# The last down-projection block of a decoder step: tokens stationary, the closing layer norm inside it

## The reference

```
x = layer_norm(ALPHA * x + h @ w_out, ln1_g, ln1_b)
u = relu(x @ w_up)
y = layer_norm(ALPHA * x + (u * u) @ w_down, ln2_g, ln2_b)

def layer_norm(x, g, b):
    mu = mean(x);  var = mean(square(x - mu))
    return (x - mu) * rsqrt(var + 1e-5) * g + b
```

## Time and profile before

| | |
|---|---|
| median of 3 runs | 2955.85 us |
| span of the profiled execution | 2953.3 us |
| PE busy | 2803.1 us (95%) |
| DVE busy | 1887.3 us (64%) |
| ACT busy | 842.9 us (29%) |
| POOL busy | 207.3 us (7%) |
| last sum of block 31 starts | 2906.40 us |
| last store issued | 2950.38 us |

### The profile page before, as it was taken

How to read it: one execution, slowest core, us unless ns; L and a number is a source line. 1 busy time by engine, 2 the same in 40 slices (tenths; PEclk the granted TensorE clock), 3 DMA queues, 4 the chain that set the end, 5 groups by cost and what they waited for, 6 DMA issues and landing times. The chain is left out here.

```text
span 2953.3 us, 58897 instructions
## 1 busy us (share of the span) xinstructions
PE 2803.1 (95%) x25775; PEld 2658.4 (90%) x25775; DVE 1887.3 (64%) x2204; ACT 842.9 (29%) x1226; POOL 207.3 (7%) x226
## 2 busy tenths in 40 slices
PE   7999999999999887899899999999999999999995
PEld 7998889888887665899789999999999999999994
DVE  3264555455553685536877777777777777777775
ACT  2221222122212355213533233232232322322321
POOL 2011101110110321001000000000000000000003
PEclk9999999999999899999999999999999999999997
DMA  9489999999999722445122232332323323323222
GB/s 343 154 314 402 410 374 412 411 400 394 413 396 340 246 79 82 104 132 138 51 79 86 86 114 71 103 106 67 115 84 88 109 72 107 101 71 115 79 94 89
DMA packets 340851, 548.62 MB, mean 186 GB/s; under 512 B 20940, under 2 KB 244781, under 8 KB 330019
## 3 DMA queue, kind: packets, MB, share of 16 engines
q1 hardware_dynamic: 263682, 334.37, 34.0%
q0 software_dynamic: 13872, 141.28, 11.8%
q10 hardware_dynamic: 63040, 69.21, 6.9%
HBM read 508.96 MB, written 35.84 MB: 184 GB/s over the span
## 5 line engine op out<-in xcount | busy, mean ns | idle before, releaser
L2129 DVE SCALAR_TENSOR_TENSOR base<-big_G,base 128x544 f32<-128x544 f32 x512 | 369.6, 722 | 244.3 <-PE big_G L1964 244.3
L449 PE MATMUL prj_G<-prj_xh,prj_wh 128*128 128x280 f32 x1696 | 504.0, 297 | 20.8 <-DVE prj_wl L692 13.9
L451 PE MATMUL prj_G<-prj_xh,prj_wl 128*128 128x280 f32 x1696 | 498.5, 294 | 0.0
L450 PE MATMUL prj_G<-prj_xl,prj_wh 128*128 128x280 f32 x1696 | 497.8, 294 | 0.0
L699 DVE STREAM_TRANSPOSE prj_kT<-base 128x4096 f32<-128x4096 f32 x64 | 284.5, 4445 | 258.3 <-PE prj_S L482 258.3
L2041 ACT ACTIVATE wh<-raw 128x1024 fp32r<-128x1024 f32 x227 | 239.4, 1059 | 652.8 <-PE big_G L1964 542.8
L1962 PE MATMUL big_G<-ff_uh,wh 128*128 128x272 f32 x1360 | 392.3, 288 | 3.6 <-DVE base L2129 3.5
L1963 PE MATMUL big_G<-ff_ul,wh 128*128 128x272 f32 x1360 | 393.5, 289 | 0.0
L1964 PE MATMUL big_G<-ff_uh,wl 128*128 128x272 f32 x1360 | 393.4, 289 | 0.0
L449 PEld LDWEIGHTS prj_G<-prj_xh,prj_wh 128*128 128x128 f32 x1696 | 322.9, 190 | 46.3 <-issue 34.5
L2116 DVE TENSOR_TENSOR wl<-raw,wh 128x1024 fp32r<-128x1024 f32 x227 | 277.0, 1220 | 86.3 <-ACT wh L2041 86.3
(11 more groups left out here) (418 smaller groups left out, 6097.2 us busy)
## 6 DMA issues: line engine op xcount, KB each, us to landing
prj_v_nat<-in_cache_v SPq DMA_DIRECT2D x242, 512.0 KB, 7.6
raw<-in_w_down SPq DMA_DIRECT2D x128, 512.0 KB, 4.4
raw<-in_w_up SPq DMA_DIRECT2D x120, 512.0 KB, 4.4
prj_raw<-in_w_in ACTq DMA_DIRECT2D x103, 512.0 KB, 17.6
raw<-in_w_out SPq DMA_DIRECT2D x16, 1024.0 KB, 7.1
prj_scratch<-prj_stage ACTq DMA_DIRECT2D x53, 280.0 KB, 9.3
out_xr<-x_scratch SPq DMA_DIRECT2D x16, 544.0 KB, 4.0
base<-in_cache_v SPq DMA_DIRECT2D x14, 512.0 KB, 7.2
```

Of the source, the lines that this page charges most:

```text
L449: mm(out, w_hi[:, k, m], xh[:, k0 + k, cols], start=(first and k == 0), stop=False)
L450: mm(out, w_hi[:, k, m], xl[:, k0 + k, cols], start=False, stop=False)
L451: last = mm(out, w_lo[:, k, m], xh[:, k0 + k, cols], start=False, stop=(end and k == nk - 1))
L2129: V.scalar_tensor_tensor(out, G[2 + t % 2][:, :, 0:HALF_M], 1.0 / ALPHA, out, ALU.mult, ALU.add).then_inc(y_done, 1)
```

## The change

The first 31 blocks stay as they are. The last block's down product is done by `down_last`, with the tokens stationary: for each of the four prompt token tiles t and each quarter d of the features (512 columns, one PSUM bank), six float32r matmuls with 512 moving columns of w_down, and behind them four float32 matmuls that turn the four pieces of `y` into the same bank, against `ident_a`, the identity times ALPHA. The bank thus holds the whole ALPHA * x + u2 @ w_down, with tokens on partitions, and no add on VectorE is needed. The fourth weight piece has buffers of its own (`fourth_h`, `fourth_l`).

The 32 samples are done ahead of it by `samples` in plain float32, with the four feature quarters on four groups of 32 partitions of one bank (8 matmuls of 512 columns, 16 turns); their mean and variance over the four quarters are made by two one-column matmuls against `select` (`over_quarters`).

`phase_end` is gone. Its work is done tile by tile behind `down_last`, with four output tiles in place of two. Gain and offset, and their quarters for the samples (ten loads), are issued on SP right after the last weight load, and land in the space of `xh`. The banks of tiles 0 and 2 are one set, of 1 and 3 the other; tile t (from 2) waits for the norm of tile t - 2. VectorE's order per tile is: last two banks' statistics, moments, scale, first two banks' statistics of the next tile, gain. GpSimd adds the offset for tiles 0 to 2. For tile 3, ScalarE normalises four quarters, VectorE does gain and offset of each, and SP stores each.

```diff
+            def samples():
+                pe.wait_ge(relu_done, NBLK)
...
+                pe.wait_ge(y_done, KT * LAST_BLK)
+                for k in range(FB):
+                    for d in range(DOWN):
+                        mm(SAMPLE[NS * d:NS * (d + 1), :], u2[:, k, NT * P:TM], down_raw(d)[:, k, :], start=(k == 0), stop=False)
+                pe.wait_ge(end_act, ACT_AT["ident_a"])
+                for j in range(4):
+                    for d in range(DOWN):
+                        last = mm(SAMPLE[NS * d:NS * (d + 1), j * P:(j + 1) * P], y[:, 4 * d + j, NT * P:TM], ident_a, start=False, stop=(j == 3))
+            def down_last(base):
+                samples()
+                pe.wait_ge(low_done, NLOW + LAST_BLK)
...
+                for t in range(NT):
+                    if t >= 2:
+                        pe.wait_ge(end_act, ACT_AT[f"norm {t - 2}"])
+                    for d in range(DOWN):
+                        if t == 0:
+                            pe.wait_ge(lo_done, base + d + 1)
+                        if t == 1 and d == 3:
+                            pe.wait_ge(end_dve, DVE_AT["scale s"])
...
+                        for k in range(FB):
+                            mm(bank, uh[:, k, tokens(t)], w_hi[:, k, :], start=(k == 0), stop=False)
+                            mm(bank, ul[:, k, tokens(t)], w_hi[:, k, :], start=False, stop=False)
+                            mm(bank, uh[:, k, tokens(t)], w_lo[:, k, :], start=False, stop=False)
+                        for j in range(4):
+                            last = mm(bank[:, j * P:(j + 1) * P], y[:, 4 * d + j, tokens(t)], ident_a, start=False, stop=(j == 3))
+                        last.then_inc(down_ps, 1)
+                        if t == 0 and d == 2:
+                            pe.wait_ge(end_act, ACT_AT["rows"])
+                            pe.wait_ge(end_dve, DVE_AT["moments s"])
+                            over_quarters(0, mv_s[:, 0:1])
+                        if t == 1 and d == 0:
+                            pe.wait_ge(end_dve, DVE_AT["square s"])
+                            over_quarters(1, mv_s[:, 3:4])
-            down(NBLK - 1, base, base)
+            down_last(FIRST + NCH * (NBLK - 2))
```

On ScalarE:

```diff
-            high(base + 3, BY_FREE[3], 2 * NBLK - 2, downs=downs + 20)
+            ac.wait_ge(raw_full[BY_FREE[3]], 16 * (2 * NBLK - 2))
+            ac.wait_ge(up_done, DOWN + UP * (NBLK - 2))
+            A(fourth_h, Q[BY_FREE[3]], ACT.Copy).then_inc(hi_done, 1)
+            A(ident_a, ident[:, :], ACT.Copy, scale=ALPHA).then_inc(end_act, 1)
...
+            ac.wait_ge(sample_ps, PE_AT["rows"])
+            A(rows, SAMPLE, ACT.Copy).then_inc(end_act, 1)
+            ac.wait_ge(sample_ps, PE_AT["var"])
+            A(mv_s[:, 4:5], MEAN[:, 1:2], ACT.Sqrt, bias=eps).then_inc(end_act, 1)
+            deviation(0)
+            ac.wait_ge(end_dve, DVE_AT["scale s"])
+            A(out_s, rows, ACT.Identity, scale=mv_s[:, 4:5], bias=mv_s[:, 5:6]).then_inc(end_act, 1)
+            normalise(0)
+            for t in (1, 2):
+                deviation(t)
+                normalise(t)
+            deviation(3)
+            ac.wait_ge(end_dve, DVE_AT["scale 3"])
+            for d, cols in enumerate(QUARTERS):
+                A(out[3][:, cols], X[1][d], ACT.Identity, scale=mv[:, 6:7], bias=mv[:, 7:8]).then_inc(end_act, 1)
```

On VectorE and GpSimd:

```diff
+            def scale(t):
+                s = 4 * (t % 2)
+                dv.wait_ge(end_act, ACT_AT[f"sd {t}"])
+                step(V.reciprocal(mv[:, s + 2:s + 3], mv[:, s + 2:s + 3]))
+                V.scalar_tensor_tensor(mv[:, s + 3:s + 4], mv[:, s:s + 1], -1.0, mv[:, s + 2:s + 3], ALU.mult, ALU.mult).then_inc(end_dve, 1)
...
+            scale(0)
+            statistics(1, (0, 1))
+            dv.wait_ge(end_act, ACT_AT["norm s"])
+            V.tensor_tensor(out_s, out_s, gain_s, ALU.mult).then_inc(end_dve, 1)
+            dv.wait_ge(end_dve, DVE_AT["gain s"])
+            V.tensor_tensor(out_s, out_s, offset_s, ALU.add).then_inc(end_dve, 1)
+            times_gain(0)
+            for t in (1, 2):
+                step(statistics(t, (2, 3)))
+                moments(t)
+                scale(t)
+                statistics(t + 1, (0, 1))
+                times_gain(t)
+            step(statistics(3, (2, 3)))
+            moments(3)
+            scale(3)
+            for d, cols in enumerate(QUARTERS):
+                dv.wait_ge(end_act, ACT_AT[f"norm 3.{d}"])
+                V.tensor_tensor(out[3][:, cols], out[3][:, cols], gain[:, cols], ALU.mult).then_inc(end_dve, 1)
+                dv.wait_ge(end_dve, DVE_AT[f"gain 3.{d}"])
+                V.tensor_tensor(out[3][:, cols], out[3][:, cols], offset[:, cols], ALU.add).then_inc(end_dve, 1)
...
+            po.wait_ge(up_done, DOWN + UP * (NBLK - 2))
+            G_.memset(eps, LN_EPS).then_inc(end_pool, 1)
+            for i in range(2):
+                G_.tensor_tensor(part_sum[:, NS * i:NS * (i + 1)], ident[:, 2 * NS * i:2 * NS * i + NS], ident[:, 2 * NS * i + NS:2 * NS * (i + 1)],
+                                 ALU.add).then_inc(end_pool, 1)
...
+            for t in range(NT - 1):
+                po.wait_ge(end_dve, DVE_AT[f"gain {t}"])
+                G_.tensor_tensor(out[t], out[t], offset, ALU.add).then_inc(end_pool, 1)
```

More of the change, by code:

```diff
@@ L1900, in phase_ff, with over @@
         PRODUCTS = ((0, B11), (1, B21), (3, T4), (3, T2), (0, T1), (2, T3), (1, B22))
+        NT, WIDE = 4, 512
+        def over(name, shape, at, dt=F32):
+            return nc.alloc_sbuf_tensor_at("ff_" + name, shape, dt, offset=at)
+        gain, offset = (over(f"vec{i}", [P, D], big["xh_at"] + 4 * i * D)[:, :] for i in range(2))
+        gain_s, offset_s, rows, out_s = (over(f"sample{i}", [P, WIDE], big["xh_at"] + 8 * D + 4 * i * WIDE)[:, :] for i in range(4))
+        ident_a, select, part_sum, mv, mv_s, eps = (
+            over(x, [P, n], big["xh_at"] + 8 * D + 16 * WIDE + 4 * at)[:, :]
+            for x, n, at in (("ident_a", P, 0), ("select", P, P), ("part_sum", 96, 2 * P), ("mv", 8, 3 * P), ("mv_s", 8, 3 * P + 8), ("eps", 1, 3 * P + 16)))
@@ L1920, in tile, with down_raw, tokens @@
             return (t + KH) % KT if b == 0 else t
+        def down_raw(d):
+            return flat(Q[BY_FREE[d]]).rearrange("p (k n) -> p k n", k=FB)
+        def tokens(t):
+            return slice(P * t, P * (t + 1))
         @block.sync
@@ new lines, in _, with statistics, moments @@
+            dv.wait_ge(hi_done, base + 4)
+            V.tensor_tensor(fourth_l, Q[BY_FREE[3]], fourth_h.bitcast(F32), ALU.subtract).then_inc(lo_done, 1)
+            step = Chain(dv, dve)
+            def statistics(t, banks):
+                for d in banks:
+                    dv.wait_ge(down_ps, KT * LAST_BLK + DOWN * t + d + 1)
+                    ins = V.bn_stats(stats[:, d, :], X[t % 2][d])
+                return ins
+            def moments(t):
+                s = 4 * (t % 2)
+                V.bn_aggr(mv[:, s:s + 2], flat(stats[:, :, :])).then_inc(end_dve, 1)
@@ new lines, in _ @@
+            dv.wait_ge(small_in, 16 * 2 * (1 + DOWN))
+            dv.wait_ge(end_act, ACT_AT["rows"])
+            step(V.bn_stats(stats_s[:, 0, :], rows))
+            V.bn_aggr(mv_s[:, 0:2], stats_s[:, 0, :]).then_inc(end_dve, 1)
+            statistics(0, (0, 1))
+            dv.wait_ge(sample_ps, PE_AT["mean"])
+            dv.wait_ge(end_dve, DVE_AT["moments s"])
+            step(V.tensor_tensor(mv_s[:, 2:3], mv_s[:, 0:1], MEAN[:, 0:1], ALU.subtract))
+            V.scalar_tensor_tensor(mv_s[:, 3:4], mv_s[:, 2:3], mv_s[:, 2:3], mv_s[:, 1:2], ALU.mult, ALU.add).then_inc(end_dve, 1)
@@ new lines, in _ @@
+            step(statistics(0, (2, 3)))
+            moments(0)
+            dv.wait_ge(end_act, ACT_AT["sd s"])
+            step(V.reciprocal(mv_s[:, 4:5], mv_s[:, 4:5]))
+            V.scalar_tensor_tensor(mv_s[:, 5:6], MEAN[:, 0:1], -1.0, mv_s[:, 4:5], ALU.mult, ALU.mult).then_inc(end_dve, 1)
+            scale(0)
[3 more added lines that the diff above has]
+            dv.wait_ge(end_dve, DVE_AT["gain s"])
```

165 lines of the change are left out of this document (72 added, 93 removed), and 3 rows, old and new, of the table DVE_AT.

## The result

The changed kernel takes 2938.81 us (median of 4 runs, 2929.57 to 2944.21), the one before 2958.26 (4 runs, 2951.85 to 2960.85; the three given above and one more). The ratio is 0.9928, with a 95% interval of 0.9901 to 0.9956: by it about 21 us less, by the two medians 19.5. Forecast were 23.9 less, a ratio of 0.9919.

A forecast was written before the change was run, and what follows sets the result against it. TensorE bounds the feed-forward phase; behind it VectorE and GpSimd take turns for 46.2 us. Handover, block, a 9.05 us norm loop and last tile end at 2929.45 instead of 2953.3, 23.9 less: 2932.0 on the median, range 2924 to 2938.

The forecast's parts named there:

- Handover: Before the last block's down product: the samples' matmuls run in TensorE's gap; block starts at 2880.45, 0.35 us later than before.
- The hidden loads: Ten gain and offset loads, issued on SP behind the last weight load, 15 us ahead of the closing norm: costed at nothing.
- The block: Last block's down product: 24 matmuls at 0.226 and 16 turns at 0.12, 7.35 us a tile, 29.4 for four.
- rival 2: Turns in the last block and samples: each costs 0.107 us more, everything 3.0 later, time 2935.0; chance 0.07.
- The clock: Start of the last block: the dip to the 1.2 GHz level after TensorE's gap stays, costing 1.6 us.
- The hold: Closing norm: the next tile's two-SBUF-operand scale on VectorE waits until GpSimd's offset ends, making a loop of 9.05 us a tile.
- Last tile: Tile 3 after its scale: first quarter's norm 0.6, eight VectorE pieces 5.5, last store 2.9 us, ending at 2929.45.
- rival 1: Closing norm: scale and offset run side by side without a hold, TensorE is the bound, time 2925.1; chance 0.11.
- 3: Last block: the clock stays at 1.2 GHz throughout, the block takes 54.8 us, time 2949.4; chance 0.05.
- 4: Last block: stationary loads no longer overlap the matmuls, 86 us in place of 29.4, time 2982, slower; chance 0.02.
- What was said to prove me wrong: Scales taking 0.16 beside a running offset, TensorE waiting microseconds for norm 1 or samples' moments, or block clock 0.5 over 4 us.
- What was said to prove me right: Block start near 2880.5, matmuls every 0.226, turns 0.11 to 0.12, scales ending with offsets, offsets 9.05 apart, about 6 us last.

The follow-up runs named there:

- e6: Changed kernel with a one-operand scale and three of four turns per quarter left out in tiles 1 to 3: tail 47.39 us, against 54.55 for the changed kernel.
- e9: Changed kernel with the prompt tiles' turns in TensorE's transpose mode, ahead of the float32r matmuls, two-operand scale kept: tail 51.74 us against 54.55.
- e2: Changed kernel with the samples' matmuls waiting for the low half of u, so TensorE idles as before the change: tail 58.05 us against 54.55.
- e4: Changed kernel with the last tile normalised, multiplied, added by GpSimd and stored whole instead of in pieces: tail 59.30 us against 54.55.
- e1: Changed kernel with each tile's scale using one SBUF tensor operand, the other a per-partition scalar: tail 51.75 us against 54.55.
- e7: Changed kernel with the prompt tiles' turns in transpose mode and the one-operand scale: tail 45.82 us against 54.55.
- e3: Changed kernel with three of four turns per quarter left out in tiles 1 to 3, 36 of 64: tail 53.30 us against 54.55.
- e10: As e8, but in the last tile all four centring pieces come before the four finishing ones: tail 45.22 us, ratio 0.9892 to the kernel before.
- e8: As e7, with the last tile's norm on VectorE alone, centring and finishing pieces interleaved: tail 45.24 us, ratio 0.9896 to the kernel before.
- e5: Changed kernel with VectorE alone doing the prompt tiles' norm, without ScalarE's norm and GpSimd's additions: tail 50.56 us, ratio 0.9932 to the kernel before.

## Why the prediction was right, and where it was 2.4 us off

By its own steps, all from the anchor:

- *Handover.* Block start 3.2, measured 3.6: right. The samples' eight matmuls took 1.92 us and not 1.0 to 1.3, for the reason below, but most of that lay under the wait for `ident_a`; their turns took 1.0 instead of 0.5, and that, with `ident_a` 0.1 early, is the 0.4. TensorE's gap was filled.
- *The hidden loads.* Costed at nothing, and nothing shows: no wait for them stands ahead of any instruction. No run moves them back.
- *The block.* The step that failed: "20 fp32 matmuls of 129 columns took 2.47 us, so 0.12 each at most". The x20 counts ten matmuls. A plain fp32 matmul leaves two rows in the trace, as the x8 for four turns shows, and costs about twice what I read: 0.23 for 128 columns. So a tile takes 9.15 us instead of 7.35. It is rival 2 (chance 0.07), whose size, 0.107 more a turn, was right; e6 (0.225 a turn) and e9 (0.11 once the turn is one row) show it. The Trainium skill (FP8 and Floating Point Precision, "TensorE Precision Notes") gives true fp32 four passes, by which, as an estimate, 128 columns at 2.4 GHz would be 0.21 us; the trace agrees (0.225), and my reading of the earlier trace rows against it was wrong. The same miscount gave the samples' matmuls, priced from the x8 row, which is four matmuls. In the pace the miscount cost nothing, as rival 2 had worked out, but only by a narrow margin: a tile of 9.15 is 0.2 shorter than the loop of the hold.
- *The clock.* I kept a dip of 1.6 us, and there was none; e2 shows why. It hid most of the dearer first tile: gain 0 started at 20.0, predicted 18.2. From the block's start to gain 0 it was 16.4 where I had 15.0 with the dip and 13.4 without: 3.0 more, 24 x 0.107 = 2.6 of it for turns and the rest for matmuls every 0.232 instead of 0.226 (36 of them) and the two small products of the samples. So the dip that did not come offset the step that failed: without this luck the miss would have been 4.0 and not 2.4 us. With 0.4 from the handover and less 1.6 of dip that is the 1.8. (e9, with cheap turns, starts gain 0 2.9 earlier.)
- *The hold.* Right in mechanism and nearly in size: all three scales end within 0.02 of an addition's end; the loop is 9.34 instead of 9.05. The differences are the norm, which is two instructions of 1024 columns here, 2.30 instead of 2.06, and the addition (4.59, 4.58 and 4.50 instead of 4.50). Over two rounds that is the other 0.6. Scale 3 ended at 45.6, predicted 43.2: 1.8 + 0.6 = 2.4, the whole miss.
- *Last tile.* From scale to last piece 6.2, predicted 6.1; store 2.7, predicted 2.9. e4 confirms the worth of it, 4.75.
- *Rivals 1, 3 and 4.* e1 shows what rival 1 would have looked like, and it was not the case; its price was wrong too, since it counted on TensorE's 7.35 a tile: without the hold the tail is 51.75, where rival 1 had 2922.5 - 2877.3 = 45.2, which only e7's block comes near. The clock was 1.00 (3; its 54.8 us from 2880.45 would end at 2935.25, not 2936.1). 512-column matmuls start every 0.23 with a load each (4; the block before had 192 loads, not 160).

What was said to prove me wrong did not occur. What was said to prove me right did, with additions 9.34 apart for 9.05, but for one item: "turns at 0.11 to 0.12". Eight rows in 1.05 us, 0.13 each, would almost have satisfied it on a hasty reading; the start of the next quarter does not.

By the ratio, 0.9928 of 2955.85 is 2934.6 us, inside the range (2924 to 2938); the median of 2938.81 as it stands is 0.8 above it, from runs in which the kernel before took 2958.26, not 2955.85. The offset of the profiled execution (10.65 us at the anchor) shows what a single profile can't tell: by the two spans the gain would have been 10.9 us. Why the phases ahead of the anchor take longer in one execution than in another stays open; the rate of one stretch does not tell it, since e3 moves 410 GB/s from 600 to 800 us and has its anchor as late as the kernel after, at 2887.99.

## What to carry to other kernels

Before a row prices an operation, count its instructions against the code: xN in a trace is not always N of the program's. And look whether the kernel before already does the same work in a cheaper form. Where two loops of nearly one length share a stage, an experiment on either shows little, and only both together show the gain (2.8 and 2.8 us alone, 8.7 together). When runs differ upstream by as much as the change is worth, measure from an anchor that both kernels have, and ask after every won microsecond what comes next: here the hold, then TensorE, then the chain of gain, statistics and norm, and at last the stores.

## What the runs showed of the hardware

- A plain fp32 matmul of 128 columns costs 0.225 us at the 2.4 GHz level and shows as two rows; the same turn in transpose mode costs 0.11, one row (e9, e7; 0.115 in the norm of the kernel before), and float32r matmuls can be summed on top of it in the bank. The Trainium skill (TensorE: Matmul & The Clock Gate, "Terms") calls that mode four times faster for FP32, without saying than what; against the plain fp32 turn it was twice here.
- VectorE with two SBUF operands is held while GpSimd's addition runs even when it works on one element a partition (2.69 us for 0.16 in the kernel after). With a per-partition scalar in place of one tensor it takes 0.21 beside it (e1). With one operand in PSUM and one in SBUF, 512 columns take 0.68 beside a running addition (e10) and 0.74 to 0.75 without one (e8, e5).
- 3.5 us without work on TensorE brought the 1.2 GHz level for about 3 us (e2); with the samples' 1.9 us of plain fp32 matmuls and their turns in that gap the clock stayed at 1.00.
